# Reordering the start of the expert stream: when slot 0 is weighed, and where attention's exponentials stand

## The chip, the cores and the metric

One core of a Trainium2 chip runs the whole kernel. The metric is the device time of one execution in microseconds. An engine runs its own list of instructions in order and waits on semaphores for the others: PE (TensorE) multiplies, DVE (VectorE) and ACT (ScalarE) compute elementwise, POOL (GpSimd) issues the indirect transfers, SP issues the plain ones.

## The reference, cut to what matters

Two transformer blocks over 256 tokens of width 1024. The first is differential attention and a linear recurrence. The second mixes an HGRN2 recurrence with sparse attention (compressed, selected and window branch), adds a layer of retrieved experts, and ends in a gated embedding. With 256 tokens the selected and the window branch see all earlier tokens. What counts here is the expert layer, which handles 128 tokens at a time:

```python
q = (xt @ wq).reshape(128, 8, 2, 128)                 # 8 heads
s = einsum('thcd,hckd->thck', q, sub_keys)            # 2 x 128 key scores a head
top_s, top_i = top_k(s, 16)
cand = top_s[:, :, 0, :, None] + top_s[:, :, 1, None, :]
best_s, best_c = top_k(cand.reshape(128, 8, 256), 16)
expert = i1 * 128 + i2                                # from best_c and top_i
w = softmax(best_s)
act = gelu(einsum('thkd,td->thk', u[expert], xt))
out = einsum('thk,thkd->td', w * act, v[expert])
```

Each token reads 8 x 16 = 128 rows of u and of v, 8 KB for the pair, out of a table of 16384 pairs. The kernel computes all in 32-bit floats.

## The kernel before, in words

Tokens lie on the 128 partitions, in two tiles. An expert *slot* is one expert for each token of a tile: 128 slots a tile, 256 in all (g = 0 to 255), 16 slots a head. A slot goes through these steps, each on its engine and ordered by semaphores:

1. POOL (L602) waits for the slot's expert numbers (`chosen`) and for its buffer (`row_used`), and issues an indirect transfer of 128 rows of u and v, 1.05 MB. There are eight buffers (`ig, kT, spare, tail, rg (named xc_rg in the trace), gl, ga, sm`), so the transfer of slot g + 8 waits until PE has done the sum of slot g. Slots 0, 1 to 7, and 8 on wait for the first, second and third `chosen`; slots 4 and 7 also wait for other users of their buffers.
2. DVE (`dot`, L2282) multiplies the rows of u with the normed tokens and sums.
3. ACT (`weigh`, L1569, L1575, L1583) takes the Gelu, multiplies it with the probability (it waits for `prob_made` at the first slot of a head) and scales the identity with it into one of four diagonal matrices.
4. PE (`expert_sum`, L1127) multiplies the diagonal with the rows of v and adds in PSUM (two matmuls of 512 columns, each in two passes).

The choice of a head's 16 experts (`choose`, L2186 on) is a generator of 19 short steps on DVE. Step 12 (`SHIFT_STEP` = 11, counted from 0) writes the shifted scores, for which ACT's `top_exp` (L1547) waits; the last steps invert the sum (it waits for `top_exp`) and make the probabilities. Within its first steps, `first_experts` gives the numbers for slots 0 to 7 early. Head 0 is chosen whole before slot 0's dot. The other heads' steps are spread between dots by `choice_rate`: two steps in each of slots 0 to 9, none in 10 and 11, then by a pattern of 16.

What is left of the second tile's mixer is also put between slots, by lists written out by hand: on PE in `second_tokens(g)`, behind sum g; on ACT in the loop over `weigh(b)`, in `if last == ...`; on DVE in the loop over `dot(g)`. An attention block (number b, of four heads) goes `att_scores` (PE, L849), `att_biased` (DVE, L1944 to L1948: bias, maximum, shift), `att_exps` (ACT, L1428), `att_turn` (PE, L858), `att_move` (ACT, L1435), `att_values` (PE, L871), `att_out` (DVE). Blocks 2 and 3 fall in the stretch that the change touches. The second tile's recurrence goes `recurrence_out` (PE, L983, L988), `recurrence_moved` (ACT, L1444), four squares with sums and a root (ACT, L1558, L1561), `recurrence_scaled` and `recurrence_gate` (DVE). A query part is L1084, its scores L1095; ACT moves them at L1530 and L1539. PE does the scores of blocks 2 and 3 ahead of sum 0.

ACT computes Exp, Sqrt, Gelu and Silu from tables; the trace shows an ACT_TABLE_LOAD where the function changes from one to another of these. Copy and Square come without one.

Of the kernel before, what the change touches and what calls it, by code (L numbers as in the profile page):

```python
# [172 lines left out]
def choice_rate(g):  # L173

    if g < 12:
        return 2 if g < 10 else 0
    return (2, 2, 1)[(g - 12) % TOPK % 3] if (g - 12) % TOPK < 12 else 0


# [21 lines left out]
def two_blocks(nc, x, wall, cols, rows, lambdas, sub_keys, peer_uv, out):  # L201
    with ExitStack() as ctx:
# [410 lines left out]
        def _(pe):  # L613
# [229 lines left out]
            def att_scores(b, part=range(8)):  # L843
                t, w, heads = STEPS2[b]
                for i, h in enumerate(heads):
                    if i not in part:
                        continue
                    half = slice(h // REP * DH, (h // REP + 1) * DH)
                    ins = nc.tensor.matmul(score2(att_psum[b], b)[:, i, :], nT3[half, h % REP, t * P:(t + 1) * P],  # L849
                                           nT3[half, 4 + w, 0:(t + 1) * P], start=True, stop=True)  # L850
                if len(heads) - 1 in part:
                    ins.then_inc(s["att_full"], 1)
# [262 lines left out]
            query_part(2, range(2))  # L1115
            pe.wait_ge(s["o_moved"], NT)
            att_scores(2)
            pe.wait_ge(s["proj_moved"], OUT_AT["hg"] + 2)
            att_scores(3)

            def expert_sum(g):
                t, n = g // TILE_SLOTS, g % DIAGS
                pe.wait_ge(s["diag_made"], g + 1)
# [10 lines left out]
            def second_tokens(g):  # L1134
# [3 lines left out]
                    query_part(2, (2, 3))  # L1138
                elif g in (2, 4):
                    query_part(2, (g + 2, g + 3))  # L1140
                elif g == 3:
                    att_turn(2)
                elif g in (5, 6):
                    att_values(2, range((g - 5) * 2, (g - 5) * 2 + 2))
                elif g == 7:
                    query_scores(2)
                elif g == 12:
# [126 lines left out]
        def _(act):  # L1274
# [167 lines left out]
            def recurrence_moved(t):  # L1442
                act.wait_ge(s["o_full"], t + 1)
                nc.scalar.activation(at2.o[:, t * HALF:(t + 1) * HALF], pa[:, t * D:t * D + HALF], ACT.Copy)\  # L1444
                    .then_inc(s["o_moved"], 1)
# [106 lines left out]
            scores_moved(1)  # L1552
            recurrence_gate_moved(1)
            top_exp(0)
            recurrence_moved(1)
            act.wait_ge(s["o_moved"], NT)
            for h in range(HG_HEADS):
                ins = nc.scalar.activation(diag[:, h * P:(h + 1) * P], at2.o[:, HALF + h * P:HALF + (h + 1) * P], ACT.Square,  # L1558
                                           accum_out=st2[:, 12 + h:13 + h])
            step(ins)  # L1560
            nc.scalar.activation(st2[:, 4:8], st2[:, 12:16], ACT.Sqrt, bias=eps_col, scale=1.0 / P)\  # L1561
                .then_inc(s["o_std"], 1)

            def weigh(b):

# [45 lines left out]
            for b in range(SLOTS // BATCH):  # L1611
                weigh(b)
                last = (b + 1) * BATCH - 1
                while head_at < NT * PEER_HEADS and dot_of_step((head_at - 1) * CHOICE_TURN + SHIFT_STEP) < last:
                    top_exp(head_at)
                    head_at += 1
                if last == 2:
                    att_exps(2)
                if last == 5:
                    att_move(2)  # L1620
                if last == 6:
                    queries_moved(2)
                if last == 9:
                    att_exps(3)
                    scores_moved(2)
                if last == 14:
                    att_move(3)
# [42 lines left out]
        def _(dve):  # L1670
# [507 lines left out]
            def choose(head):  # L2178
# [5 lines left out]
                def done(ins):  # L2184
                    before[0] += 1
                    ins.then_inc(s["choice_step"], 1)  # L2186

                def settled():
                    dve.wait_ge(s["choice_step"], before[0])

                scores = pscores[t][:, n * 2 * NKEYS:(n + 1) * 2 * NKEYS].rearrange("p (c n) -> p c n", c=2)
                v3 = v16.rearrange("p (c k) -> p c k", c=2)
                i3 = i16.rearrange("p (c k) -> p c k", c=2)
# [38 lines left out]
                        done(V.match_replace(pairs, best[:, where], pairs, LOWEST))  # L2232
                        yield
                settled()
                mine = probs[:, head * TOPK:(head + 1) * TOPK]
                V.tensor_scalar(mine, best, best[:, 0:1], None, ALU.subtract).then_inc(s["top_shift"], 1)
                V.tensor_scalar(places_i[:, 0:TOPK], best_at, 4, None, ALU.logical_shift_right)
                done(V.tensor_scalar(places_i[:, TOPK:2 * TOPK], best_at, TOPK - 1, None, ALU.bitwise_and))
                yield
                settled()  # L2240
                done(V.tensor_copy(places, places_i))
# [25 lines left out]
                    V.tensor_scalar(pieces_at[:, 0:LAST], last, 2.0, None, ALU.mult)  # L2267
                    V.tensor_scalar(pieces_at[:, LAST:2 * LAST], last, 2.0, 1.0, ALU.mult, ALU.add)
                V.tensor_copy(experts[:, head * TOPK + new:(head + 1) * TOPK], keys_f[:, new:TOPK]).then_inc(s["chosen"], 1)
                dve.wait_ge(s["top_exp"], head + 1)  # L2270
                done(V.reciprocal(prob_sum[:, head:head + 1], prob_sum[:, head:head + 1]))
                yield
                settled()
                V.tensor_scalar(mine, mine, prob_sum[:, head:head + 1], None, ALU.mult).then_inc(s["prob_made"], 1)
                assert before[0] == (head + 1) * (CHOICE_STEPS - 1)
                yield

# [33 lines left out]

            dve.wait_ge(s["rows_loaded"], 32)
            norm_gained(0)
            for _ in choose(0):
                pass
            between = choices()
            for g in range(SLOTS):
                dot(g)
                for _ in range(choice_rate(g)):
                    next(between, None)  # L2320
                if g == 1:
                    att_biased(2)
                if g == 2:
                    recurrence_scaled(1)
                    recurrence_gate(1)
                if g == 7:
                    att_biased(3)
                if g == 11:
                    att_out(2)
                if g == 24:  # L2330
                    att_out(3)
# [160 lines left out]
```

## Time and profile before

| what | us |
|---|---|
| median of 3 timed runs | 1103.23 (1101.94 to 1103.65) |
| the profiled execution | 1100.11 |
| its span, first to last instruction | 1098.4 |
| PE busy | 1011.0 (92%) |
| DVE busy | 646.7 (59%) |
| ACT busy | 453.9 (41%) |
| POOL busy | 310.1 (28%) |
| indirect transfers (q0) | 269.89 MB, 59.4% of 16 engines |

All times in the text are microseconds from the span's start. The span falls into the part before the expert rows (to about 397), the stream of the expert rows (to about 1068) and a tail of some 30. Shares of busy time are means over these. A row of a timeline gives the start, the time from the start of the first to the end of the last of its instructions, the engine, the line, the operation, what is written and read, the count, and in brackets the idle time before it with the engine that ended it. PE's busy time contains modelled ends. The slices of the page are 27.5 us each.

### The profile page before, as it was taken

How to read it: one execution, taken by the hardware profiler on the slowest of the kernel's cores; microseconds unless marked ns; L12 is line 12 of the kernel's file. 1: busy time of each engine (PE TensorE's matmuls, PEld its weight loads, DVE VectorE, ACT ScalarE, POOL GpSimd, SP SyncE). 2: the span in 40 equal slices, each digit the busy share in tenths (PEclk: the TensorE clock that was granted, in tenths of full speed). 3: DMA queues.
4: the chain of work that ended last, by engine and by line, in shares of the span. 5: the costliest groups of instructions: out<-in, count | busy, mean ns of one | idle time of the engine just before them, and what ended most of it. 6: DMA issues, size and time to landing. Idle time of an engine off the chain costs nothing.

```text
span 1098.4 us, 10613 instructions
## 1 busy us (share of the span) xinstructions
PE 1011.0 (92%) x3533; PEld 563.2 (51%) x3533; DVE 646.7 (59%) x1497; ACT 453.9 (41%) x1167; POOL 310.1 (28%) x307
## 2 busy tenths in 40 slices
PE   9999999999999999999899788998898988877778
PEld 8887458544686466554354343554433432322224
DVE  4525255305443479786776676767567668668443
ACT  1143255311254148554544544445344354344333
POOL 3000000001000024543444344454434334443430
PEclk9999999999999999999999899999899999999999
DMA  9426432244626459999999999999999999999990
GB/s 345 149 110 230 153 122 109 77 154 172 230 87 236 166 215 419 423 407 409 422 421 420 422 420 421 420 421 421 421 422 421 421 422 421 422 422 422 420 403 30
DMA packets 46679, 347.26 MB, mean 316 GB/s; under 512 B 5056, under 2 KB 6464, under 8 KB 9120
## 3 DMA queue, kind: packets, MB, share of 16 engines
q0 software_dynamic: 37584, 269.89, 59.4%
q1 hardware_dynamic: 9040, 76.69, 18.4%
q8 instruction: 28, 0.46, 0.2%
q14 instruction: 27, 0.22, 0.1%
HBM read 345.25 MB, written 1.05 MB: 315 GB/s over the span
## 4 chain that ended last, share of the span: by engine, by line
PE 58%; DMA 29%; DVE 6%; ACT 5%; issue 1%; SPq 0%; DVEq 0%
DMA tail<-in_peer_uv,small 20%; PE pp L1127 15%; PE pp L648 8%; PE pp L684 5%; DMA xc_rg<-in_peer_uv,small 4%; PE pp L680 4%; PE pp L666 3%; DMA ig<-in_peer_uv,small 3%; PE pp L809 3%; PE pp L787 3%; PE pp L829 3%; DMA spare<-in_peer_uv,small 2%; PE pp L1019 2%; DVE tail L2282 2%; PE pp L1223 2%; PE pa L1084 2%
## 5 line engine op out<-in xcount | busy, mean ns | idle before, releaser
L1569 ACT ACTIVATE small<-small 128x1 f32<-128x1 f32 x256 | 51.6, 201 | 309.5 <-DVE small L2282 308.2
L1583 ACT ACTIVATE diag<-ident,small 128x128 f32<-128x128 f32 x256 | 102.8, 402 | 8.4
L1127 PE MATMUL pp<-xc_rg,diag 128*128 128x512 f32 x128 | 64.4, 627 | 21.2 <-ACT diag L1583 21.1
L1575 ACT ACTIVATE small<-small 128x1 f32<-128x1 f32 x256 | 75.4, 294 | 9.3
L1127 PE MATMUL pp<-sm,diag 128*128 128x512 f32 x128 | 64.2, 626 | 11.8 <-ACT diag L1583 11.8
L602 POOL DMA_INDIRECT ig<-in_peer_uv,small x32 | 43.8, 1367 | 104.7 <-PE pa L1084 54.0
L1127 PE MATMUL pp<-tail,diag 128*128 128x512 f32 x128 | 61.9, 606 | 10.8 <-ACT diag L1583 10.8
L1127 PE MATMUL pp<-kT,diag 128*128 128x512 f32 x128 | 63.0, 615 | 9.0 <-ACT diag L1583 9.0
L1127 PE MATMUL pp<-ig,diag 128*128 128x512 f32 x128 | 63.7, 621 | 8.3 <-ACT diag L1583 8.2
L1127 PE MATMUL pp<-spare,diag 128*128 128x512 f32 x128 | 62.3, 609 | 8.5 <-ACT diag L1583 8.5
L648 PE MATMUL pp<-hT,ring 128*128 128x256 f32 x320 | 69.6, 379 | 0.0
L1127 PE MATMUL pp<-ga,diag 128*128 128x512 f32 x128 | 61.6, 603 | 6.3 <-ACT diag L1583 6.3
L1127 PE MATMUL pp<-gl,diag 128*128 128x512 f32 x128 | 62.4, 610 | 4.3 <-ACT diag L1583 4.3
L648 PEld LDWEIGHTS pp<-hT,ring 128*128 128x128 f32 x320 | 60.8, 190 | 8.3
L547 POOL IOTA tail<- 128x256 int32 x1 | 0.3, 342 | 226.2 <-DVE xs L1883 226.2
L2282 DVE CUSTOM_DVE_ANT_0 tail<-tail,xc_rg 128x1024 f32<-128x1024 f32 x32 | 39.2, 1225 | 34.1 <-DMA tail<-in_peer_uv,small 34.0
L2282 DVE CUSTOM_DVE_ANT_0 spare<-spare,xc_rg 128x1024 f32<-128x1024 f32 x32 | 39.2, 1224 | 32.8 <-DMA spare<-in_peer_uv,small 32.7
L684 PE MATMUL pp<-hT,ring 128*128 128x256 f32 x256 | 58.1, 381 | 0.0
L2282 DVE CUSTOM_DVE_ANT_0 xc_rg<-xc_rg 128x1024 f32<-128x1024 f32 x32 | 39.2, 1225 | 29.0 <-DMA xc_rg<-in_peer_uv,small 28.9
L2282 DVE CUSTOM_DVE_ANT_0 ig<-ig,xc_rg 128x1024 f32<-128x1024 f32 x32 | 39.1, 1223 | 27.0 <-DMA ig<-in_peer_uv,small 27.0
L2282 DVE CUSTOM_DVE_ANT_0 kT<-kT,xc_rg 128x1024 f32<-128x1024 f32 x32 | 39.2, 1224 | 26.8 <-DMA kT<-in_peer_uv,small 26.7
L602 POOL DMA_INDIRECT xc_rg<-in_peer_uv,small x32 | 33.9, 1060 | 64.1 <-PE pp L1127 58.5
(493 smaller groups left out, 1924.7 us busy)
## 6 DMA issues: line engine op xcount, KB each, us to landing
ring<-in_wall SPq DMA_DIRECT2D x31, 2048.0 KB, 7.8
ring<-in_wall SPq DMA_DIRECT2D x4, 512.0 KB, 7.1
ring<-in_wall SPq DMA_DIRECT2D x1, 1280.0 KB, 9.6
xs<-in_x SPq DMA_DIRECT2D x2, 512.0 KB, 3.8
post_g<-in_rows POOLq DMA_DIRECT2D x2, 512.0 KB, 8.9
tail<-in_wall SPq DMA_DIRECT2D x1, 1024.0 KB, 11.2
kT<-in_wall SPq DMA_DIRECT2D x1, 1024.0 KB, 13.2
lt<-in_sub_keys SPq DMA_DIRECT2D x1, 1024.0 KB, 7.4
```

What stands on the lines that cost most here:

```text
L602: nc.gpsimd.indirect_dma_start(out=rows_uv[page_of(g)], out_offset=None, in_=peer_uv, in_offset=bass.IndirectOffsetOnAxis(ap=experts[:, g: ...
L648: ins = nc.tensor.matmul(buf[:, c, :], mine, raw3[:, k, :] if name == "xl0" else h3[:, k, :], start=(k == 0), stop=(k == KC - 1))
L666: ins = nc.tensor.matmul(buf[:, t, 0:width], h3[:, k, t * P:(t + 1) * P], w[:, k, 0:width], start=(k == 0), stop=(k == KC - 1))
L680: ins = nc.tensor.matmul(buf[:, t, :], h3[:, k, t * P:(t + 1) * P], w[:, k, :], start=(k == 0), stop=(k == KC - 1))
L684: ins = nc.tensor.matmul(flat[:, c, :], w[:, k, c * P:(c + 1) * P], h3[:, k, :], start=(k == 0), stop=(k == KC - 1))
L787: ins = nc.tensor.matmul(bufs[c][:, t, :], gl3[:, k, t * P:(t + 1) * P], wo[c][:, k, :], start=(k == 0), stop=False)
L809: ins = nc.tensor.matmul(bufs[c][:, t, :], h3[:, k, t * P:(t + 1) * P], wo[c][:, k, :], start=False, stop=(k == KC - 1))
L1127: ins = nc.tensor.matmul(acc[t][:, c, :], diag[:, n * P:(n + 1) * P], rows_uv[page_of(g)][:, D + c * HALF:D + (c + 1) * HALF], start=False ...
L1569: nc.scalar.activation(acts[:, at:at + BATCH], dots[:, at:at + BATCH], ACT.Gelu_apprx_tanh)\
L1575: ins = nc.scalar.activation(wk[:, g % LAG:g % LAG + 1], acts[:, g % LAG:g % LAG + 1], ACT.Copy, scale=probs[:, g:g + 1])
L1583: nc.scalar.activation(diag[:, n * P:(n + 1) * P], ident[:, :], ACT.Copy, scale=wk[:, g % LAG:g % LAG + 1]).then_inc(s["diag_made"], 1)
L2282: V.tensor_tensor_reduce(out=row_u, in0=row_u, in1=xn[t], scale=1.0, scalar=0.0, op0=ALU.mult, op1=ALU.add, accum_out=dots[:, g % LAG:g % ...
```

## The change

Four things are reordered; the arithmetic is the same.

- The probabilities of head 0 are made in step 12 of its choice, right behind the shifted scores; the rest of that choice (places, expert numbers for slots 8 to 15) goes on behind the dots of slots 0 and 1. The other heads' steps come two in each of slots 2 to 11.
- ACT weighs slot 0 before it moves the second tile's recurrence. The squares and the root for it follow slot 3 (squares are written to `h3` instead of `diag`), on DVE the scaling and gating come at slot 5 instead of 2.
- PE does the scores of block 3 behind sum 1 instead of ahead of sum 0, the turn of block 2 behind sum 5 (was 3), its values behind sums 8 and 9 (were 5 and 6).
- ACT takes the exponentials of block 2 behind slot 3 (was 2), its move behind 7 (was 5), the exponentials of block 3 behind 8 (was 9), where by the new `choice_rate` the exponential of head 1 stands too. On DVE the bias of block 2 comes at slot 2 (was 1), its output at 13 (was 11).

```diff
 def choice_rate(g):
     if g < 12:
-        return 2 if g < 10 else 0
+        return 2 if g >= 2 else 0

 # PE
             att_scores(2)
-            pe.wait_ge(s["proj_moved"], OUT_AT["hg"] + 2)
-            att_scores(3)
...
-                elif g == 3:
+                elif g == 1:
+                    pe.wait_ge(s["proj_moved"], OUT_AT["hg"] + 2)
+                    att_scores(3)
+                elif g == 5:
                     att_turn(2)
-                elif g in (5, 6):
-                    att_values(2, range((g - 5) * 2, (g - 5) * 2 + 2))
+                elif g in (8, 9):
+                    att_values(2, range((g - 8) * 2, (g - 8) * 2 + 2))

 # ACT
             top_exp(0)
-            recurrence_moved(1)
-            act.wait_ge(s["o_moved"], NT)
-            for h in range(HG_HEADS):
-                ins = nc.scalar.activation(diag[...], at2.o[...], ACT.Square, accum_out=...)
-            step(ins)
-            nc.scalar.activation(st2[:, 4:8], st2[:, 12:16], ACT.Sqrt, ...).then_inc(s["o_std"], 1)
+            def last_recurrence_std():       # the same, squares into h3[:, h, P:2 * P]
...
+                if last == 0:
+                    recurrence_moved(1)
-                if last == 2:
+                if last == 3:
+                    last_recurrence_std()
                     att_exps(2)
-                if last == 5:
-                    att_move(2)
                 if last == 6:
                     queries_moved(2)
+                if last == 7:
+                    att_move(2)
+                if last == 8:
+                    att_exps(3)
                 if last == 9:
-                    att_exps(3)
                     scores_moved(2)

 # DVE, in choose(head), step 12
                 V.tensor_scalar(mine, best, best[:, 0:1], None, ALU.subtract).then_inc(s["top_shift"], 1)
                 V.tensor_scalar(places_i[:, 0:TOPK], best_at, 4, None, ALU.logical_shift_right)
                 done(V.tensor_scalar(places_i[:, TOPK:2 * TOPK], best_at, TOPK - 1, None, ALU.bitwise_and))
+                if head == 0:
+                    probabilities()
...
 # DVE, the loop over slots
-            for _ in choose(0):
-                pass
+            first_head = choose(0)
+            for _ in range(SHIFT_STEP + 1):
+                next(first_head)
             for g in range(SLOTS):
                 dot(g)
+                if g == 1:
+                    for _ in first_head:
+                        pass
                 for _ in range(choice_rate(g)):
                     next(between, None)
-                if g == 1:
+                if g == 2:
                     att_biased(2)
-                if g == 2:
+                if g == 5:
                     recurrence_scaled(1)
                     recurrence_gate(1)
-                if g == 11:
+                if g == 13:
                     att_out(2)
```

`probabilities()` waits for ACT's exponential of the head, inverts the sum and multiplies.

## Rows read from the trace of the kernel before

**Rows 1.** The page's slices: GB/s moved in each of 40.

```profile
GB/s 345 149 110 230 153 122 109 77 154 172 230 87 236 166 215 419 423 407 409 422 421 420 422 420 421 420 421 421 421 422 421 421 422 421 422 422 422 420 403 30
```

**Rows 2.** Stretches: length, busy PE, PEld, DVE, ACT, POOL, clock, DMA share, GB/s.

```profile
486.00:498.00 12.00, 12.00 (x35) 5.77 (x34) 9.84 (x32) 9.55 (x26) 6.20 (x5) 1.00 0.98 361
498.00:1045.00 547.00, 476.42 (x1344) 218.46 (x1342) 372.35 (x917) 251.90 (x722) 235.87 (x210) 0.98 1.01 421
```

**Rows 3.** Timeline of POOL: issues of slots 0, 2, 3 and 35.

```profile
396.80 1.05 POOL L602 DMA_INDIRECT ig<-in_peer_uv,small  x1 [54.03 <-PE pa L1084]
...
400.30 0.94 POOL L602 DMA_INDIRECT spare<-in_peer_uv,small  x1 [0.30 <-issue]
401.54 0.94 POOL L602 DMA_INDIRECT tail<-in_peer_uv,small  x1 [0.30 <-issue]
...
488.70 1.70 POOL L602 DMA_INDIRECT tail<-in_peer_uv,small  x1 [1.64 <-PE pp L1127]
```

**Rows 4.** Landing by tile, of the issues at 396.80, 400.30, 401.54, 486.12, 488.70.

```profile
DMA to landing us min/median/max: 5.7/5.7/5.7
...
DMA to landing us min/median/max: 11.5/11.5/11.5
...
DMA to landing us min/median/max: 14.5/14.5/14.5
...
DMA to landing us min/median/max: 7.6/7.6/7.6
...
DMA to landing us min/median/max: 9.6/9.6/9.6
```

**Rows 5.** Timeline of DVE: places, dots 0 and 1, bias, dot 2.

```profile
404.08 0.18 DVE L2241 CAST nq<-nq 128x32 f32<-128x32 uint32 x1
...
407.16 1.22 DVE L2282 CUSTOM_DVE_ANT_0 ig<-ig,xc_rg 128x1024 f32<-128x1024 f32 x1
...
409.36 1.21 DVE L2282 CUSTOM_DVE_ANT_0 kT<-kT,xc_rg 128x1024 f32<-128x1024 f32 x1
...
411.70 1.42 DVE L1944 SCALAR_TENSOR_TENSOR xc_rg<-mask,pa 128x256 f32<-128x256 f32 x4
...
414.61 1.22 DVE L2282 CUSTOM_DVE_ANT_0 spare<-spare,xc_rg 128x1024 f32<-128x1024 f32 x1
```

**Rows 6.** Timeline of ACT: first square, table loads, diagonal of slot 3.

```profile
408.43 0.31 ACT L1558 ACTIVATE diag<-xl 128x128 f32<-128x128 f32 x1
...
411.34 1.28 ACT L1569 ACT_TABLE_LOAD   x1
...
416.86 1.28 ACT L1428 ACT_TABLE_LOAD   x1
...
420.25 1.28 ACT L1569 ACT_TABLE_LOAD   x1
...
422.11 0.40 ACT L1583 ACTIVATE diag<-ident,small 128x128 f32<-128x128 f32 x1
```

**Rows 7.** Timeline of PE: scores, sum 0, turn of block 2, sums 4, 10.

```profile
409.68 2.96 PE L849 MATMUL pa<-vv 64*128 64x256 f32 x16
413.71 1.98 PE L1127 MATMUL pp<-ig,diag 128*128 128x512 f32 x4 [1.07 <-ACT diag L1583]
...
424.38 1.04 PE L858 MATMUL pa<-ident,xc_rg 128*128 128x128 f32 x8
425.25 1.88 PE L1127 MATMUL pp<-xc_rg,diag 128*128 128x512 f32 x4
...
441.89 1.98 PE L1127 MATMUL pp<-spare,diag 128*128 128x512 f32 x4 [1.70 <-ACT diag L1583]
```

**Rows 8.** One stretch as in rows 2, and PE's sums behind two waits.

```profile
620.00:621.00 1.00, 0.21 (x1) 0.21 (x2) 0.00 (x0) 0.87 (x4) 0.00 (x0) 0.50 1.06 442
...
620.79 3.78 PE L1127 MATMUL pp<-sm,diag 128*128 128x512 f32 x4 [4.85 <-ACT diag L1583]
...
904.03 2.92 PE L1127 MATMUL pp<-kT,diag 128*128 128x512 f32 x4 [2.87 <-ACT diag L1583]
```

More of the change, by code:

```diff
@@ L1554, in _ @@
             top_exp(0)
-            recurrence_moved(1)
-            act.wait_ge(s["o_moved"], NT)
-            for h in range(HG_HEADS):
-                ins = nc.scalar.activation(diag[:, h * P:(h + 1) * P], at2.o[:, HALF + h * P:HALF + (h + 1) * P], ACT.Square,
-                                           accum_out=st2[:, 12 + h:13 + h])
-            step(ins)
-            nc.scalar.activation(st2[:, 4:8], st2[:, 12:16], ACT.Sqrt, bias=eps_col, scale=1.0 / P)\
-                .then_inc(s["o_std"], 1)
+            def last_recurrence_std():
+                act.wait_ge(s["o_moved"], NT)
+                for h in range(HG_HEADS):
+                    ins = nc.scalar.activation(h3[:, h, P:2 * P], at2.o[:, HALF + h * P:HALF + (h + 1) * P], ACT.Square,
+                                               accum_out=st2[:, 12 + h:13 + h])
+                step(ins)
+                nc.scalar.activation(st2[:, 4:8], st2[:, 12:16], ACT.Sqrt, bias=eps_col, scale=1.0 / P)\
+                    .then_inc(s["o_std"], 1)
             def weigh(b):
@@ L2189, in settled, with sum_inverted, probabilities @@
                     dve.wait_ge(s["choice_step"], before[0])
+                mine = probs[:, head * TOPK:(head + 1) * TOPK]
+                def sum_inverted():
+                    dve.wait_ge(s["top_exp"], head + 1)
+                    done(V.reciprocal(prob_sum[:, head:head + 1], prob_sum[:, head:head + 1]))
+                def probabilities():
+                    sum_inverted()
+                    settled()
+                    V.tensor_scalar(mine, mine, prob_sum[:, head:head + 1], None, ALU.mult).then_inc(s["prob_made"], 1)
                 scores = pscores[t][:, n * 2 * NKEYS:(n + 1) * 2 * NKEYS].rearrange("p (c n) -> p c n", c=2)
@@ L2234, in choose @@
                 settled()
-                mine = probs[:, head * TOPK:(head + 1) * TOPK]
                 V.tensor_scalar(mine, best, best[:, 0:1], None, ALU.subtract).then_inc(s["top_shift"], 1)
@@ L2269, in choose @@
                 V.tensor_copy(experts[:, head * TOPK + new:(head + 1) * TOPK], keys_f[:, new:TOPK]).then_inc(s["chosen"], 1)
[L2270 to L2274, printed above, removed]
+                if head > 0:
+                    sum_inverted()
+                    yield
+                    settled()
+                    V.tensor_scalar(mine, mine, prob_sum[:, head:head + 1], None, ALU.mult).then_inc(s["prob_made"], 1)
                 assert before[0] == (head + 1) * (CHOICE_STEPS - 1)
```

## The prediction, made before the changed kernel was run

> **What bounds the kernel now.** I read the slices first. From slice 16 on the core moves about 421 GB/s without a break [rows 1], and the same view by stretches says so with numbers: 421 GB/s over the 547 us from 498 to 1045 [rows 2]. That is the stream of the 256 expert rows, 1.05 MB each, so one row every 2.49 us. An engine that waits in this part, and PE, ACT and DVE all do, waits for a transfer that is already as fast as the others. So the end is set by when the stream starts, by the bytes, and by every microsecond in which the DMA engines have nothing to do. There is one such place: from 486 to 498 the rate is 361 [rows 2], which is 12 x (1 - 361/421) = 1.7 us of lost transfer time. All that a better order can win is there, for the stream's start (first issue at 396.80 [rows 3]) comes before the first instruction that the change moves.
>
> Why is time lost there? A row's buffer is asked for again when its expert sum on PE is done: eight buffers, and the issue of row g+8 waits for sum g. PE has its last wait at 441.89 [rows 7] and is busy for all of the 12 us from 486 [rows 2]: with a query part or the like between its sums it falls behind the stream's 2.49 us a row, and the issues come later and later against the landings. The time from issue to landing tells how full the queue is: 14.5 us early on, 7.6 us for the issue at 486.12, and 9.6 us for the next at 488.70, which so lands 4.6 us after it where 2.49 would be its turn; a row into an empty queue took 5.7 [rows 3, 4]. So up to the issue at 488.70 PE sets the pace, and from its landing on the DMA engines do. A microsecond lost on PE before 488 should be a microsecond at the end; a microsecond won there brings at most the 1.7.
>
> **The start of the stream, part by part.** I call the sums e0, e1 and so on.
>
> First head's probabilities. Before, DVE has the shifted values just ahead of the places (404.08), and the first dot begins at 407.16 [rows 5]. Row 0 had landed at 396.80 + 5.7 = 402.5 [rows 3, 4]. Now reciprocal and product come right behind ACT's exponential (some 0.9 us for the crossing to ACT and back and two small instructions), so dot 0 runs from about 404.7 and dot 1 (row 1 lands about 405.7) ends about 407.1. The rest of head 0, 404.08 to 407.1, moves behind dot 1 and ends about 410. The signal for rows 8 and on comes 3 us later, at 410, but row 8 also waits for e0 (about 413), so nobody is held up.
>
> First slot weighed early. ACT weighs slot 0 at once (its diagonal is ready at about 407), then moves the recurrence at 407.8 as before. The squares and the root, 408.43 to 411.34, 2.91 us [rows 6], no longer stand before e0. PE does its eight score matmuls for block 2 from 409.68, half of the sixteen in 2.96 us [rows 7], and starts e0 at about 411.2 instead of 413.71: 2.5 us won. Low bound 1.07 (only the idle before it), high bound 2.96 less the half.
>
> e1 to e3. From e0 to e4 PE worked without a pause before: 413.71 to 425.25, 11.54 us, with the turn of block 2 (424.38 to 425.25, 0.87) in it [rows 7]. Now the turn goes behind e5 and the scores of block 3 (1.48) come in: 12.15. PE is through with e3 at 411.2 + 12.15 = 423.4, with some tenths of draining 423.8.
>
> **The new wait: e4.** Between the weighing of slot 3 and of slot 4 ACT now has the four squares, the root with its table, the exponentials of block 2 with theirs, and the Gelu table again. Each piece has its row: 2.91 (408.43 to 411.34), 3.39 (416.86 to 420.25), and 2.26 from the Gelu load to the end of the diagonal (420.25 to 422.51) [rows 6]: 8.56 us. When does it start? Slot 3 needs dot 3. Row 3 lands at 401.54 + 14.5 = 416.0; row 2 at 400.30 + 11.5 = 411.8 [rows 3, 4]. DVE: dot 2 until 413.0, two steps of the choice (1.1: dot 0 begins at 407.16 and takes 1.14 until its sum is read, dot 1 begins at 409.36 [rows 5]), then the bias of block 2 (411.70 to 414.61, 2.9 [rows 5]) until 417.0, dot 3 until 418.2, its diagonal on ACT 1.0 later, 419.2. Add 8.56: the diagonal for e4 is there at 427.8. At the very least, with dot 3 right at its landing, 426.9. So PE waits 4.0 us (423.8 to 427.8; bounds 2.9 and 4.5), and e4 starts 2.55 us later than its 425.25. Queued behind on ACT are slots 5 to 7 and the query move, which then have room. The head start of 2.5 is used up and as much again is lost.
>
> e5 to e10. Before: 425.25 to 441.89, 16.64 us, of which 1.70 idle right before e10 [rows 7], for ACT's exponentials of block 3. Now: the work 14.94, the turn 0.87 more, and of that idle time something stays, for the exponentials of block 3 now stand in front of slot 9, beside the second head's exponential. That saves two table loads (one pair), 2.6 us of ACT, but ACT has also to wait for the query part behind e4 and the turn behind e5, both late. Bounds 0 and the 1.70 of before, taken 1.0. Sum 16.8: e10 at 444.6 against 441.89, 2.7 late. From here both orders give PE the same work. DVE is some 3 us behind at slots 12 to 14 (head 2 waits for the moved scores), but PE needs those dots 4 us later than that; it costs nothing.
>
> **The clock.** The granted clock was 0.5 for some us behind the wait that ended at 620.79 (4.85 us idle), and the four matmul passes of a sum took 3.78 there for the 1.98 of e0 [rows 7]; behind a wait of 2.87 us (904.03) they took 2.92 [rows 8]. A wait of 4.0 us lies between, so I expect the lower level (1.2 GHz) once more. Price: 0.94 by the second row, 1.8 by the first, 0 if it stays up. I take 0.94.
>
> The Trainium skill ("ScalarE: Activation LUTs", What ACT_TABLE_LOAD costs) counts a drain of about 1.4 us beside the 1.28 of each load. Rows 6 show no room for one: from the load at 408.43 + 2.91 = 411.34 to the diagonal of slot 3 the loads follow the work before them with no gap, and the squares, the root and its load together take no more than 2.91. By the page, as an estimate, the three loads between slots 3 and 4 would make the new wait 4.1 us longer. I go by the rows.
>
> **The sum.** PE late 2.6 (between the 2.55 at e4 and the 2.7 at e10), clock 0.9: 3.5 us at the issue that was at 488.70, and so at the end. The profiled execution took 1100.11 (span 1098.4 and 1.7 around it); it would be 1103.6. The median of the timed runs is 1103.23, 3.1 above it; I add the same 3.5 and forecast 1106.7.
>
> **Rivals.**
> The queue swallows it. The stall makes the issues of rows 12 to 18 late while 10 us of transfers are queued, and the loss at 486 to 498 may be no matter of lateness: DVE is then busy without a gap (dots made up behind block 4's bias), and the issue at 488.70 took 1.70 us where others take 0.94 [rows 3]. If generating is blocked by DVE, and not late, the same 2 us are lost whether PE is late or not, and the empty queue's 5.7 leaves room of 7.6 - 5.7 = 1.9 us. Then 3.5 - 1.9 or less arrives, 0 to 1.6: about 1104.1. For it: the 9.6 us with so little ahead in the queue. Against: at 7.6 us, with three rows asked for, the queue is near its floor just where the rate falls. The Trainium skill ("SBUF — State Buffer", SBUF: two separate sides) says that a DVE instruction in a two-port mode keeps GpSimd from writing descriptors until it ends; the long issue times agree, but no row here shows the lost rate to come from it.
>
> The hole is filled (the other side). If ACT comes to slot 4 before PE is done with e3, by squares and root in its idle time before dot 3 (ACT has 4 us free there, but the order written puts them behind slot 3), the 2.5 us of the head start would stay, and the 1.70 before e10 go as well. The queue would be deeper by 4 and the 1.7 us of lost transfer vanish: 1103.2 - 1.7 = 1101.5. It decides from the point where the wait before e4 is under 2.5 us; the 8.56 of rows 6 speak against it.
>
> Drains as the page has them: 4.1 us more, 1110.8.
>
> **Chances.** The stall reaches the end 0.62, range for it alone 1105.2 to 1108.8 (2.0 to 5.6: e4 0.9 earlier and full clock, or the clock at 1.8 and e9's wait at 1.7). Swallowed 0.18. Filled 0.16. Drains 0.04. Two tenths of a per cent, 2.2 us, is about what a measurement of this kernel tells from no change. Slower by that: 0.58 of the first and the 0.04, 0.62. Same: 0.04, 0.18 and half of the filled case, 0.30. Faster needs more than the 1.7 that can be won, so only chance of measurement or a cause unseen: 0.08. Range 1102.5 to 1108.8.
>
> **What would show it.** Right: e0 at about 411, a wait of PE before e4 of 3 to 4.5 us ended by ACT's diagonal, ACT going squares, root, exponentials between slots 3 and 4, e10 at 444 to 445, a clock of 0.5 about 428, and less than 421 GB/s earlier than 486 and longer, together 5 us of transfer lost. Wrong: e4 before 426; or e10 at 444.6 and the lost transfer still 1.7; or the landing time of rows 12 to 20 falling below 7 us with the rate at 421, which would mean that the queue has more room than I give it.

## The result, and the profile after

| | before | after |
|---|---|---|
| median of the timed runs | 1100.70 (16 runs) | 1105.50 (16 runs, 1103.73 to 1110.47) |
| ratio | | 1.0041 (95% interval 1.0032 to 1.0050) |
| profiled execution, its span | 1100.11, 1098.4 | 1106.15, 1104.3 |

The kernel became slower, by 4.8 us in the medians and by 6.0 between the two profiled executions. The forecast was 1106.7 with a range of 1102.5 to 1108.8. It was built on a median of before of 1103.23 from three runs; over 16 runs the median is 1100.70. So the predicted difference (+3.5) was too small by 1.3, and the base was too high by 2.5. The two errors go against each other, and that the forecast came within 1.2 is in part luck. Counted from 1100.70, the same additions give 1104.2 and, for the stall reaching the end, 1102.7 to 1106.3; 1105.50 lies in that too.

The slices of the page show where the time went. In slices 16 to 19 (414 to 525 in after, 412 to 522 in before) after moves 387, 372, 420 and 402 GB/s where before moved 419, 423, 407 and 409 [rows 1]; from there on both run at about 421.

```profile
GB/s 349 152 110 218 152 142 87 81 148 171 231 84 255 145 245 387 372 420 402 421 421 421 422 421 421 420 421 420 422 420 422 421 421 418 420 422 422 421 403 28
```

The stretches of after (length, then busy us of PE, PEld, DVE, ACT and POOL, granted clock, DMA share, GB/s), to be held against [rows 2]:

```profile
486.00:498.00 12.00, 12.00 (x31) 5.63 (x31) 11.33 (x36) 6.90 (x18) 5.53 (x5) 1.00 1.01 404
410.00:420.00 10.00, 10.00 (x43) 6.14 (x42) 6.62 (x19) 1.02 (x4) 4.65 (x5) 1.00 1.00 419
420.00:430.00 10.00, 4.72 (x23) 3.02 (x22) 9.76 (x30) 9.72 (x29) 2.94 (x2) 0.95 1.02 424
430.00:440.00 10.00, 10.00 (x39) 5.71 (x38) 9.34 (x23) 5.02 (x13) 2.77 (x3) 0.88 0.89 324
440.00:450.00 10.00, 9.05 (x44) 5.79 (x43) 6.82 (x25) 8.57 (x28) 4.51 (x5) 1.00 1.00 386
450.00:500.00 50.00, 50.00 (x192) 28.00 (x191) 40.15 (x104) 25.47 (x74) 21.75 (x20) 1.00 1.00 395
498.00:1045.00 547.00, 480.14 (x1354) 220.46 (x1353) 373.16 (x923) 252.85 (x724) 242.06 (x211) 0.98 1.01 420
```

PE stands still for half of 420 to 430 while ACT is full (9.72 of 10 us). The transfers feel it ten microseconds later, once the rows already asked for have run out: 430 to 440 runs at 324 GB/s, 440 to 450 at 386, 450 to 500 at 395. Priced as the prediction priced it (10 us times 1 less the rate over 421 GB/s, summed over the 66 stretches of 10 us from 400 to 1060), after loses 7.3 us of transfer time and before 1.6. The 5.7 between them is close to the difference of the profiled executions (6.0).

PE's timeline of after, from the scores of block 2 to the sum of slot 10 (start, time, operation; in brackets the idle time and what ended it):

```profile
409.32 1.99 PE L849 MATMUL pa<-vv 64*128 64x256 f32 x8
411.24 1.98 PE L1124 MATMUL pp<-ig,diag 128*128 128x512 f32 x4
...
416.66 1.99 PE L849 MATMUL pa<-vv 64*128 64x256 f32 x8
...
422.18 1.88 PE L1124 MATMUL pp<-tail,diag 128*128 128x512 f32 x4
429.34 3.45 PE L1124 MATMUL pp<-xc_rg,diag 128*128 128x512 f32 x4 [5.28 <-ACT diag L1584]
...
445.00 1.98 PE L1124 MATMUL pp<-kT,diag 128*128 128x512 f32 x4 [0.95 <-ACT diag L1584]
447.66 1.94 PE L1124 MATMUL pp<-spare,diag 128*128 128x512 f32 x4
```

Sum 0 starts at 411.24, 2.5 us before its 413.71 [rows 7]. Then PE waits 5.28 us for the diagonal of slot 4, and the sum behind that wait takes 3.45 us where others take 1.98. Sum 10 starts at 447.66, 5.8 after its 441.89.

ACT's timeline between the diagonals of slots 3 and 4 holds the reason, piece by piece as in [rows 6]: squares, the root with a table load, the exponentials with a second, the Gelu with a third. ACT is not idle between any two of them.

```profile
420.44 0.40 ACT L1584 ACTIVATE diag<-ident,small 128x128 f32<-128x128 f32 x1
420.75 0.29 ACT L1559 ACTIVATE hT<-xl 128x128 f32<-128x128 f32 x1
...
422.03 1.28 ACT L1562 ACT_TABLE_LOAD   x1
...
423.64 1.28 ACT L1428 ACT_TABLE_LOAD   x1
...
427.03 1.28 ACT L1570 ACT_TABLE_LOAD   x1
...
428.88 0.40 ACT L1584 ACTIVATE diag<-ident,small 128x128 f32<-128x128 f32 x1
```

From the start of slot 3's diagonal to the start of slot 4's it is 8.44 us. From the first square to the end of slot 4's diagonal, which is what the prediction summed up to 8.56, it is 8.53. DVE's timeline shows why the chain began late:

```profile
404.26 1.22 DVE L2300 CUSTOM_DVE_ANT_0 ig<-ig,xc_rg 128x1024 f32<-128x1024 f32 x1
...
413.51 1.23 DVE L2300 CUSTOM_DVE_ANT_0 spare<-spare,xc_rg 128x1024 f32<-128x1024 f32 x1 [3.24 <-DMA spare<-in_peer_uv,small]
...
418.62 1.22 DVE L2300 CUSTOM_DVE_ANT_0 tail<-tail,xc_rg 128x1024 f32<-128x1024 f32 x1
```

Row 2 was issued at 399.94 and landed at 413.5, 13.6 us later; before it took 11.5 [rows 4]. So dot 2 waited for it, and the bias of block 2 and dot 3 stood behind dot 2.

### The profile page after: what moved, and what is told of

Its sections match the earlier page's. It is cut to its first block, busy times and chain, and to the rows that moved or that the text cites. A ratio compares the mean times of both kernels' runs of the same rounds, so it can differ in the third digit from the quotient of the medians.

```text
span 1104.3 us, 10611 instructions
## 1 busy us (share of the span) xinstructions
PE 1015.9 (92%) x3533; PEld 564.1 (51%) x3533; DVE 646.7 (59%) x1497; ACT 450.3 (41%) x1165; POOL 311.0 (28%) x307
## 4 chain that ended last, share of the span: by engine, by line
PE 57%; DMA 30%; ACT 6%; DVE 4%; issue 2%; POOL 0%; SPq 0%; DVEq 0%; ACTq 0%
PE pp L1124 16%; DMA tail<-in_peer_uv,small 16%; PE pp L648 8%; DMA xc_rg<-in_peer_uv,small 7%; PE pp L684 5%; DMA spare<-in_peer_uv,small 5%; PE pp L680 4%; PE pp L666 3%; DMA ig<-in_peer_uv,small 3%; PE pp L809 3%; PE pp L787 2%; PE pp L829 2%; PE pp L1019 2%; PE pp L1223 2%; DVE tail L2300 1%
## 5 line engine op out<-in xcount | busy, mean ns | idle before, releaser
L1124 PE MATMUL pp<-kT,diag 128*128 128x512 f32 x128 | 65.6, 637 | 12.6 <-ACT diag L1584 12.6
L602 POOL DMA_INDIRECT ig<-in_peer_uv,small x32 | 41.4, 1294 | 103.0 <-PE pa L1084 54.0
```

The lines of the kernel that those rows point to most:

```text
L602: nc.gpsimd.indirect_dma_start(out=rows_uv[page_of(g)], out_offset=None, in_=peer_uv, in_offset=bass.IndirectOffsetOnAxis(ap=experts[:, g: ...
L1124: ins = nc.tensor.matmul(acc[t][:, c, :], diag[:, n * P:(n + 1) * P], rows_uv[page_of(g)][:, D + c * HALF:D + (c + 1) * HALF], start=False ...
```

## The experiments

Twelve more kernels were timed, each beside runs of the kernel before. Two questions were asked of them: does a late PE at the start of the stream reach the end one for one, and where does the time go that is won there? In the table "sum 11" is the start of PE's sum of slot 11 and "dot 143" the start of DVE's dot of slot 143, both counted from the first issue on POOL; "lost" is the transfer time lost from 400 to 1060, as above. These three are from one profiled execution each. In f1 and e3 the first issue came late in the execution (398.5 and 397.9 for 396.8), and 0.8 and 0.6 of their lost transfer are only that.

| kernel | sum 11 | lost | dot 143 | median | ratio (95%) |
|---|---|---|---|---|---|
| before | 47.8 | 1.6 | 388.9 | 1100.5 to 1100.9 | |
| after | 53.9 | 7.3 | 395.3 | 1105.5 | 1.0041 (1.0032, 1.0050) |
| e1_root_early | 50.7 | 5.2 | 392.7 | 1102.4 | 1.0016 (1.0006, 1.0026) |
| e2_both_early | 49.8 | 3.8 | 391.9 | 1103.3 | 1.0024 (1.0013, 1.0035) |
| e4_wait_filled | 51.3 | 4.9 | 392.1 | 1104.0 | 1.0030 (1.0018, 1.0041) |
| e3_pe_busy_3us | 49.3 | 3.2 | 390.5 | 1101.7 | 1.0006 (0.9996, 1.0015) |
| f4_pe_busy_at11 | 47.8, then + 3.4 | 4.4 | 391.9 | 1104.2 | 1.0035 (1.0021, 1.0049) |
| f1_slot0_alone | 52.8 | 7.4 | 394.6 | 1105.7 | 1.0044 (1.0031, 1.0058) |
| f2_exps_late | 45.8 | 1.2 | 388.8 | 1100.5 | 0.9996 (0.9987, 1.0005) |
| f3_spread | 45.8 | 0.9 | 388.7 | 1100.5 | 0.9998 (0.9989, 1.0008) |
| f5_pe_busy_at103 | 47.8 | | 389.1 | 1100.7 | 0.9999 (0.9989, 1.0008) |
| g1_f2_gate53 | | | 388.8 | 1100.2 | 0.9995 (0.9987, 1.0004) |
| g2_f3_gate53 | | | 388.7 | 1100.3 | 0.9993 (0.9985, 1.0002) |
| g3_before_gate53 | | | 389.1 | 1100.6 | 0.9997 (0.9988, 1.0005) |

(The "before" row gives the medians of the jobs; sum 11 of f5 is by its code, which is before's up to slot 103.)

### The wait made shorter: e1_root_early, e2_both_early

In the changed kernel, squares and root behind slot 1, where ACT has nothing to do:

```diff
-                if last == 3:
+                if last == 1:
                     last_recurrence_std()
+                if last == 3:
                     att_exps(2)
```

> The changed kernel with one thing put elsewhere: the squares and the root follow slot 1 on ACT, which is idle there for 5.9 us, and no longer slot 3; the exponentials of block 2 stay behind slot 3. Theory (the wait before e4 is ACT's chain, and it reaches the end): the chain between slots 3 and 4 falls from 8.5 to 5.6 us, the wait before e4 from 5.3 to 2.4, the granted clock stays at 1.0 there (another 1.5 us), e10 starts about 443.3 instead of 447.7, and the time falls by 4.4 from 1105.5 to about 1101. Rival (the time is lost by the other moves, the scores of block 3 or the wait before e9): the wait before e4 falls but the time stays above 1104.

e2 puts the exponentials of block 2 behind slot 2 besides, and its bias on DVE one slot earlier:

```diff
+                if last == 2:
                     att_exps(2)
...
-                if g == 2:
+                if g == 1:
```

> The changed kernel with squares and root behind slot 1, the bias of block 2 on DVE at slot 1 (DVE is idle 3.2 us for row 2 there) and its exponentials on ACT behind slot 2. Theory: no wait of more than 1 us before e1 to e8, the head start of 2.5 us is kept, e10 at about 440 (441.9 in the kernel before), and the part of the stretch from 486 to 498 at a low rate shrinks; 1099.0 to 1100.7, so up to 1.7 faster than the kernel before (1100.7) and 5 faster than the changed one. Rival (the lost 1.7 us are not a matter of PE's lateness): 1100.7, and the rate from 486 to 498 still about 360.

The wait before sum 4 shrank from 5.28 to 0.92 (e1) and to nothing (e2). But a new one came before sum 9, in PE's timeline of e1 and then of e2:

```profile
440.45 3.57 PE L1124 MATMUL pp<-kT,diag 128*128 128x512 f32 x4 [1.89 <-ACT diag L1584]
```

```profile
439.64 3.38 PE L1124 MATMUL pp<-kT,diag 128*128 128x512 f32 x4 [2.38 <-ACT diag L1584]
```

Two things make it. ACT works without a pause from the diagonal of slot 8 (433.32 in e2) to that of slot 9 (439.19), 5.87 us: a table load, the exponential of head 1, those of block 3 and the Gelu's load. And that chain could not begin sooner, for it needs dot 8, and DVE comes to dot 8 at 35.0 us behind the first issue in e2 where before came at 35.1, though its dot 0 is 2.6 earlier; DVE is busy for 33.3 of the 36 us from 404 to 440. The granted clock behind the wait of 1.89 us was 0.50 (441 to 444), and the sum took 1.6 us more. So both kernels stayed slower than before. For e2 an end ahead of before was expected, for e1 about 1101: both missed, for the head start of 2.1 us at sum 0 was lost again at slot 9. e2 ought to be better than e1 by its sum 11 and was not measurably different; their intervals overlap.

### The wait filled, and PE made late: e4_wait_filled, e3_pe_busy_3us, f4_pe_busy_at11

e4 is the changed kernel with five products that nobody uses behind sum 3, in PE's wait. e3 is the kernel before with four of them at that place, f4 with four behind sum 11:

```diff
+                elif g == 3:
+                    for _ in range(5):
+                        nc.tensor.matmul(pp[:, 0, 0], ident[:, :], lt[:, 0:HALF], start=True, stop=True,
+                                         skip_group_check=True)
```

> The changed kernel with five such matmuls behind sum 3 (4.3 us), where PE otherwise waits 5.3 us for e4's diagonal. The wait is filled with work, e4 starts at the same time. Theory: the granted clock stays at 1.0, the four passes of e4 take 1.98 instead of 3.45, e10 is 1.5 earlier and the time is 1104.0 instead of 1105.5. If the clock's share is nothing at the end: 1105.5.

> The kernel before, with four matmuls more (identity times 512 columns, into a bank that is free) behind sum 3: 3.4 us of work for PE, no change on ACT or DVE, and no idle PE whose clock could fall. Theory (each us that PE is late before slot 27's sum arrives at the end): slower by 3.4 us, 1104.1, with the rate below 421 from about 450 on. Rival (the queue swallows it): at most 1.6 slower, under 1102.3.

> The kernel before with the same four matmuls (3.4 us of PE) behind sum 11 instead of sum 3, so behind PE's last idle time (1.70 us before e10), which took up half of them in the kernel with the work behind sum 3. Theory (what counts is how late PE is behind slot 10, one for one): 3.4 slower than before, 1104.2, 4.8 to 5.2 us of transfer lost in all. Rival (the queue swallows about three quarters of any lateness, as 0.9 for 3.4 us in the timed runs of the other suggests): 0.9 slower, 1101.7.

In e4 the products take PE's wait (4.46 us in PE's timeline) and the sum behind them runs at 1.98:

```profile
424.33 4.46 PE L1143 MATMUL pp<-lt,ident 128*128 128x512 f32 x10
428.67 1.98 PE L1124 MATMUL pp<-xc_rg,diag 128*128 128x512 f32 x4
```

The clock of 429 to 433 shows the two levels. After, where PE had waited, and e4, where it had not:

```profile
429.00:433.00 4.00, 3.66 (x8) 1.88 (x9) 3.93 (x12) 1.86 (x7) 0.00 (x0) 0.58 1.01 422
```

```profile
429.00:433.00 4.00, 4.00 (x22) 2.74 (x21) 3.86 (x14) 1.75 (x7) 0.94 (x1) 1.00 1.00 418
```

Sum 11 comes 2.6 us earlier than in after: 1.5 is the clock's share (3.45 less 1.98), 1.1 is luck, for row 2 landed that much sooner in this execution. 2.4 us less transfer is lost. The median is 1.5 lower with more work on PE; the intervals of the two ratios overlap a little, so the profile carries this point more than the times do.

e3 came out less late than was expected, and the profile says why. The four products took 3.44 us, but the wait of 1.70 before sum 10 [rows 7] was gone in exchange, so at sum 11 PE was only 1.46 late; 1.6 us more transfer was lost, and the median rose by 0.9, which by its interval cannot be told from nothing. f4 puts the same products behind that wait. Nothing takes them up, 2.8 us more transfer is lost, and the median is 3.6 higher for 3.4 us of work (2.3 to 5.4 by the interval; the profiled execution alone shows 2.8 from the first issue to the end). In this place a microsecond on PE is about a microsecond at the end.

### The parts alone, and a head start: f1_slot0_alone, f2_exps_late, f3_spread

f1 has the early probabilities, slot 0 weighed first and the root behind slot 1, with attention placed as before. f2 is the kernel before with one thing moved:

```diff
                 if last == 9:
-                    att_exps(3)
                     scores_moved(2)
+                if last == 11:
+                    att_exps(3)
```

f3 is e2 with block 3 spread in the same way (its bias on DVE at slot 10, its exponentials behind slot 11).

> One part of the change alone: head 0's probabilities and slot 0 early, squares and root behind slot 1, the choice of head 1 in slots 2 to 11 as in the changed kernel; attention (scores, bias, exponentials, turn, values) where the kernel before has it. Theory (DVE is busy from 400 to 440 either way, so sum 10 depends on DVE's and ACT's order and not on when sum 0 starts): e0 about 411.4, 2.3 early, but a wait of 3 to 5 us before e10, e11 1 to 3 us later than before, with a low clock behind it; 1101.5 to 1104. Rival (the head start is worth what it wins): 1099 to 1100.

> The kernel before with the exponentials of block 3 behind slot 11 instead of slot 9 on ACT; nothing else is moved. Theory: e10 needs no wait (1.70 us before), PE is 1.7 earlier from slot 10 on and up to 1.6 us of lost transfer come back: 1099.3, against 1100.8. Rival (DVE's dots set PE's pace at slots 10 to 12): a wait shows before e11 or e12 instead, no change.

> The kernel with root and exponentials of block 2 early (waits of PE: 2.38 us before e9, and a low clock), with the bias of block 3 on DVE behind dot 10 instead of 7 and its exponentials on ACT behind slot 11 instead of 8. Theory: no wait before e9 to e12, e11 about 442.5 (446.4 there, 444.6 in the kernel before), at most 0.3 us of transfer lost up to 520; 1099.2, 1.6 faster than the kernel before. Rival: PE waits for a dot instead (DVE has no free time there), or the lost transfer at 486 to 498 stays although PE is early: 1100.8.

f1 showed the wait and the low clock that were expected, but its time lies 1.7 us above the expected range. It was as slow as the whole change, without the changed place of attention's exponentials. The head start at sum 0 is there (15.8 us behind the first issue for before's 16.9) and worth nothing, for the wait before sum 10, 1.70 before, became 4.11, and the clock fell:

```profile
445.97 3.78 PE L1127 MATMUL pp<-spare,diag 128*128 128x512 f32 x4 [4.11 <-ACT diag L1584]
```

ACT's timeline shows where the 2.41 us between the two waits come from. First f1, diagonals of slots 8, 9 and 10 and the loads between them, then the diagonals of slots 9 and 10 in before:

```profile
435.38 0.40 ACT L1584 ACTIVATE diag<-ident,small 128x128 f32<-128x128 f32 x1
435.80 1.28 ACT L1547 ACT_TABLE_LOAD   x1
...
437.42 1.28 ACT L1570 ACT_TABLE_LOAD   x1
...
439.28 0.40 ACT L1584 ACTIVATE diag<-ident,small 128x128 f32<-128x128 f32 x1
439.70 1.28 ACT L1428 ACT_TABLE_LOAD   x1
...
443.66 1.28 ACT L1570 ACT_TABLE_LOAD   x1
...
445.52 0.40 ACT L1584 ACTIVATE diag<-ident,small 128x128 f32<-128x128 f32 x1
```

```profile
435.20 0.40 ACT L1583 ACTIVATE diag<-ident,small 128x128 f32<-128x128 f32 x1
...
441.43 0.40 ACT L1583 ACTIVATE diag<-ident,small 128x128 f32<-128x128 f32 x1
```

From slot 9's diagonal to slot 10's it is 6.24 us in f1 and 6.23 in before. But slot 9's diagonal stands 40.8 us behind the first issue in f1 and 38.4 in before, 2.4 later, because the new `choice_rate` puts the exponential of head 1 (L1547) between slots 8 and 9, with a table load on either side. In before it came at 427.35, behind slot 6. ACT is not idle from slot 8 to slot 10 in f1. The head start itself was gone already at dot 8, which stands at 35.1 behind the first issue in both: the same dots, choice steps and attention steps go through DVE before it in either order. f3 shows that it is these: against e2 it has block 3's bias out of DVE's way there, and its dot 8 comes at 32.1 where e2's comes at 35.0.

f2 and f3 take the wait before sum 10 away. Here the timeline of f2, where sums 9 to 11 follow each other without a gap:

```profile
438.75 1.88 PE L1127 MATMUL pp<-kT,diag 128*128 128x512 f32 x4
440.47 1.88 PE L1127 MATMUL pp<-spare,diag 128*128 128x512 f32 x4
442.18 1.05 PE L1084 MATMUL pp<-xl,ring 128*128 128x128 f32 x8
443.07 1.88 PE L1127 MATMUL pp<-tail,diag 128*128 128x512 f32 x4
```

PE is 2.0 us ahead of before at sum 11, and the hole at 486 to 498 is closed: 423 GB/s for the 361 of [rows 2].

```profile
486.00:498.00 12.00, 11.42 (x34) 5.28 (x33) 11.14 (x33) 10.31 (x29) 5.98 (x5) 1.00 1.01 423
```

The hole closes although DVE is busier there (11.14 of 12 us for before's 9.84), so it was not DVE's work that kept the transfers back. And yet the median is that of before. The prediction took the 1.7 us of this hole for all that a better order can win; filling it won nothing that can be measured. In f2 a new hole appears at 908 to 916. The stretch in before, then in f2:

```profile
908.00:916.00 8.00, 6.64 (x15) 2.39 (x13) 7.79 (x27) 2.34 (x9) 4.05 (x4) 0.98 1.01 416
```

```profile
908.00:916.00 8.00, 6.66 (x16) 2.75 (x15) 7.80 (x25) 1.99 (x7) 4.09 (x4) 1.00 0.95 351
```

It lies behind ACT's sigmoids of the gate, which stand between slots 184 and 185 with a table load on either side, and behind which PE waits 2.87 us, with a slow sum after it, in both kernels.

### Is it given back there? g1_f2_gate53, g2_f3_gate53, g3_before_gate53, f5_pe_busy_at103

The three g kernels have the sigmoids behind slot 181, where ACT is idle for 2.5 us:

```diff
-                if last == TILE_SLOTS + 56:
+                if last == TILE_SLOTS + 53:
                     gate_moves(0)
```

f5 is f4 with its products behind slot 103.

> The kernel f2_exps_late (block 3's exponentials behind slot 11; 1100.5 us, no transfer lost at 486 to 500, some 1.6 us lost at 908 to 916) with ScalarE's sigmoids of the gate's first tokens (two of 128x512 with a table load ahead of and behind them, 3.82 us) behind slot 181 in place of slot 184. At slot 181 ScalarE has 2.54 us idle behind it, at slot 184 1.5 us. Theory 'the gain is given back at the sigmoids': TensorE's wait of 2.87 us shrinks to 1.5 or less, the rates of 908 to 916 stay at 420 GB/s, the end comes 1.6 us earlier: 1098.9 us, ratio 0.9985. Rival 'the rows had already drawn level by slot 132 (dots there stand 346 us behind the first issue in both kernels) and other bounds set the end': the rates at 908 are mended and the time stays at 1100.5 us, ratio 1.000. Rival 'the wait comes elsewhere': the wait lands at slot 182 with 2.5 us or more, the clock falls there, and the loss moves to 903 to 911: 1100.5 us or over.

> The same move of the sigmoids in f3_spread (1100.5 us; attention's exponentials and the last squares all ahead of slot 12 but spread out). 'Given back at the sigmoids': 1098.9 us. 'Drawn level before': 1100.5 us.

> The kernel before with the sigmoids behind slot 181 alone. Before loses no transfer at 904 to 918, so both theories expect no change: 1100.6 us, ratio 1.000; it separates a worth of the move itself from its worth beside a head start.

> The kernel before with four more 128x512 matmuls behind slot 103's sum (3.4 us as they took behind slot 11, where the kernel became 3.6 us slower). What is left out: nothing, their product is not used. Behind slot 103 TensorE waits 1.67 us at 670.9 and 2.49 us at 674.5 for ScalarE's diagonal. Theory 'lateness counts only where TensorE hands buffers back last': the two waits take it up, ratio 1.000 (0 to +0.5 us). Rival 'TensorE's work costs its time wherever it stands': +3.4 us, 1104.0 us.

In g1 the rate at this place is mended, though 398 GB/s at 920 to 930 shows that a part of the loss has moved:

```profile
908.00:916.00 8.00, 4.29 (x9) 1.68 (x10) 7.49 (x21) 1.87 (x7) 3.20 (x3) 0.94 1.00 411
```

The time did not follow: 1100.2, where 1098.9 was expected if the gain had been given back at the sigmoids, and g1, g2 and g3 cannot be told from before. The theory "given back at the sigmoids" falls, and "drawn level before" stands. DVE's dot of slot 143 shows it, in before, f2 and g1, with first issues at 396.80, 397.25 and 398.25:

```profile
785.71 1.22 DVE L2282 CUSTOM_DVE_ANT_0 sm<-sm,xc_rg 128x1024 f32<-128x1024 f32 x1 [3.20 <-DMA sm<-in_peer_uv,small]
```

```profile
786.06 1.23 DVE L2283 CUSTOM_DVE_ANT_0 sm<-sm,xc_rg 128x1024 f32<-128x1024 f32 x1 [3.19 <-DMA sm<-in_peer_uv,small]
```

```profile
787.06 1.23 DVE L2283 CUSTOM_DVE_ANT_0 sm<-sm,xc_rg 128x1024 f32<-128x1024 f32 x1 [3.20 <-DMA sm<-in_peer_uv,small]
```

That is 388.9, 388.8 and 388.8 behind the first issue. At slot 96 f2 was still ahead, 262.7 to before's 264.6; at slot 100 it was 0.9 ahead, at slot 128 0.1. Most of that lead is not f2's own: f5 and g3 have before's code up to slot 103, and they stood at 262.9 and 263.4 at slot 96. Held against f5, f2's dots lead by 0.8 us at slot 60 and by 0.2 to 0.3 from slot 72 on; the 2.0 that PE had won never reached them whole. The rows of a kernel that is on time all come to this point together, each dot waiting for its transfer. Every kernel that was late at sum 11 arrives here late by the same within a microsecond (the column "dot 143") and stays so to the end. The medians follow less closely (e1 is 3.8 late here and 1.5 in the median); the column is of one execution each.

The traces also hold the packets of the transfers, and these show that f2 has its lead in bytes while its rows have none. In bytes f2 is ahead of before by 1.7 us of transfer (0.7 MB) from 100 to 500 us behind the first issue, so the closed hole is there. But a row is complete only when the last of its 16 parts has landed. In before the first and the last part of a row land 0.6 us apart for slot 0, 2.8 for slot 48, 4.3 for slot 96 and 7.6 for slot 252, and the stream ends with the number of packets under way falling from 16 at 1068 to 1 at 1075. The mean rate of the 16 engines, by which the hole was priced, does not say when the last part lands. That the last parts set the pace all along the stream is a reading; no run tested it. f2's last packet of the rows ends 679.4 us behind the first issue, before's 679.3.

f5 confirms it from the other side, though not for the reason that was written down: the waits of 1.67 and 2.49 us named there lie ahead of slot 103. The products (684.00 to 687.44) make the next sum 2.1 us late, and it and the three sums behind it follow each other without the waits of 0.5 us that each of them has in before, until PE is level again:

```profile
684.00 3.60 PE L1149 MATMUL pa<-lt,ident 128*128 128x512 f32 x8
687.44 1.88 PE L1127 MATMUL pp<-ig,diag 128*128 128x512 f32 x4
...
692.59 1.88 PE L1127 MATMUL pp<-tail,diag 128*128 128x512 f32 x4
694.62 1.98 PE L1127 MATMUL pp<-xc_rg,diag 128*128 128x512 f32 x4 [0.15 <-ACT diag L1587]
```

The same 3.4 us of work cost 3.6 us behind slot 11 and nothing that can be measured behind slot 103.

## Why the prediction was right, and where its sizes were off

- **What bounds the kernel.** Right for lateness: after, e1 to e4, f1 and f4 show a late PE as lost transfer and a later end. Wrong for a gain: the step "a microsecond won there brings at most the 1.7" gave an upper bound, and the runs show nothing measurable (f2, f3). The loss at 486 to 498 is a loss of mean rate; the bytes came back in f2, the last parts of the rows came no sooner.
- **Sum 0 2.5 us earlier.** Right: 411.24 for "about 411.2".
- **The chain on ACT.** Right: 8.53 for 8.56, put together from rows of the pieces. In after there is no gap ahead of the three loads or behind them, so the drains that the page of the Trainium skill adds ("ScalarE: Activation LUTs", What ACT_TABLE_LOAD costs) are not seen here either; that rival (1110.8) is out.
- **The wait before e4.** Mis-sized: 5.28 for 4.0, above the upper bound of 4.5. The step that failed was the start of the chain: row 2 was put at its landing time of before, 11.5 us, and took 13.6. The diagonal of slot 3 was ready at 420.8 and not at 419.2. The "some tenths of draining" behind e3 had no row; in after e3 ends at 424.06 for the 423.8 taken. In e1 and e4, with the same issues ahead, row 2 took 12.0 and 12.5 us, so this term varies between executions. Sum 4 was 4.1 late, not 2.55.
- **The wait before e9.** Right in after: 0.95 for 1.0. What was not seen is that this place is the next bound: with the wait before e4 gone it grew to 1.9 to 2.4 (e1, e2) and, for sum 10 in f1, to 4.1. The prediction counted the two table loads that are saved when head 1's exponential stands beside block 3's. It did not count that the new `choice_rate` moves this exponential from slot 6, where ACT had room, to slot 8, where it has none.
- **The clock.** It fell as expected. The price was 1.47 for 0.94, by the same sum in e4, where the clock stayed up.
- **The sum.** 5.8 us late at sum 10, the clock included, for 3.5; 4.8 in the medians. Of the difference of 2.3, some 1.3 is the longer wait and 0.5 the clock; the rest is small terms between sums 4 and 10.
- **The queue swallows it.** Out. Nothing was swallowed: at 486 to 498 after still loses 0.5 us, and 6.6 before and after that stretch in 400 to 520. Its reason, DVE holding up the issues at 486 to 498, is out too: in f2 the rate is 423 there with DVE busier and an issue of 1.73 us at 487.17.
- **The hole is filled.** Its condition (a wait before e4 under 2.5 us) was met in e1 and e2, and they were still slower than before. In f2 and f3 the hole was filled and the end did not move, so this rival failed twice: at its condition in after, and in what it would have brought.

What stays open: why some parts of a row land ever later than the others, and whether that is what holds the rows in the middle of the stream. The landings were read in before only, and no run changed how a row is split. No version beat both kernels by more than the measurement tells; the least medians, g1's 1100.2 and g2's 1100.3, lie within it.

## What to carry to other kernels

Moving a step earlier on one engine buys nothing if the engine behind it is full up to the next meeting point (dot 8 here); before counting a head start, follow it to the next wait and ask whether that wait only grows. List the function switches that a new order moves along with it: one exponential moved by two slots put 2.4 us more of waiting in PE's way (f1). Price a delay and a gain apart: here 3.4 us of extra work on PE cost 3.6 at one place and 0 at another, and 2 us won at the first place brought nothing measurable. A mean transfer rate below its peak is no gain to be had until the landing of the last part of a row is seen to move. When functions with different tables are put between two links of a chain, sum their rows as one block: the block of 8.4 us was forecast within 0.1, and what was missed was when it could start.

## What the runs showed of the hardware that was not expected

- Behind PE waits of 1.89, 2.38, 4.11 and 5.28 us a sum took 3.57, 3.38, 3.78 and 3.45 us for 1.98, at a granted clock of 0.50 to 0.58. The length of the wait does not tell whether the clock falls: behind 1.70 us [rows 7] and behind 2.49 us the sum took 1.98, the latter at a granted clock of 1.00 (677 to 681 of before, below). Behind 2.24 us in g3 the sum took 1.98 and behind 2.23 us in g1, ahead of the same slot's sum, 2.94. Behind 2.87 us it cost 0.9 in before [rows 8] and more in f2 (3.68 us, at 904.47).

```profile
676.99 1.98 PE L1127 MATMUL pp<-xc_rg,diag 128*128 128x512 f32 x4 [2.49 <-ACT diag L1583]
```

- The landing time of row 2 was 11.5, 12.0, 12.5 and 13.6 us in the executions of before, e1, e4 and after, with the same issues ahead of it. A chain that starts from a landing is known no better than that.
- The 16 parts of one row's transfer land 0.6 us apart at the start of the stream (slot 0) and 7.6 us apart near its end (slot 252, before), while the mean rate stays at 421 GB/s.
- Useless products in a wait of PE kept the clock up and took 1.5 us off the sum behind it (e4).
